# Gate and up pairs of a feed-forward layer in 512-column matmuls, with other PSUM banks and a gate loop that spans three chunks

## The chip, the cores and the metric

The kernel runs on one core of one Trainium2 chip. The metric is the device time of one execution in microseconds (us). The engines of the core are named as in the profile: PE is TensorE's matmul side and PEld its weight load, DVE is VectorE, ACT is ScalarE, POOL is GpSimd, SP is SyncE, whose queue issues the weight transfers. PSUM has eight banks of 512 f32 columns on 128 partitions. Matmuls write it, and DVE and ACT read it.

## The reference, cut to what matters

The program is three transformer layers one after another on 256 tokens of width 1024: one layer with chunked attention and a recurrent branch, one with a gated delta rule, and one with block attention. Each ends in a feed-forward part. That of the first layer is gated, those of the second and third square a ReLU:

```python
D_FF = ((8 * D_MODEL // 3 + 255) // 256) * 256        # 2816
...
        hn = rmsnorm(h, norm_ffn_g[l])
        gu = hn @ w_ffn_in[l]                          # 1024 x 5632
        g, up = jnp.split(gu, 2, axis=-1)
        h = h + (jax.nn.silu(g) * up) @ w_ffn_out[l]
...
def squared_relu_mlp(hn, w_up, w_down):
    return jnp.square(jax.nn.relu(hn @ w_up)) @ w_down  # 1024 x 4096, 4096 x 1024
```

## The kernel before

All activations stay in SBUF with features on partitions and the 256 tokens along the row. All weights come from HBM in **chunks** of 1 MB (128 x 2048 f32, buffer RAW, three slots), 173 in all, and each chunk is used once. The list SEGMENTS gives their order. The segments that matter here are `fi` (22 chunks: gate and up columns of the first feed-forward part, 128 gate columns beside the 128 up columns that belong to them), `fo` (11 chunks, its output rows), `u0` and `u1` (16 chunks each, the up product of the other two), `w0` and `w1` (16 chunks each, their output rows). The prediction calls `fi` the gate stage, `u0` and `u1` the up stages, and `fo`, `w0`, `w1` the row stages.

A product of f32 precision is made of three products of a rounded type (fp32r): each operand is split into a high part and the rest. For a weight chunk, ACT writes the high part WH (`split_hi`, L365) and DVE the rest WL (`split_lo`, L374). For the normed input XH and XL are the two halves of one tile, XHL. Function `product` (L378, L379, L380) then issues WH times XH, WH times XL and WL times XH, each of 256 columns, all into the same 256 columns of PSUM. A chunk of the gate stage is 2 blocks of 128 output features times 8 blocks of 128 input features, so 16 such triples. In the up stages `multiply_wide` (L434, L436) issues two matmuls in place of three: WH times the whole of XHL in 512 columns (XH's result in one half of a bank, XL's in the other), and WL times XH in 256 columns into the second half. Such a chunk holds two banks, those that the table WIDE gives for its place modulo 3. ACT copies the second halves of both banks to SG (L1256), then DVE adds the first halves to them (L1653).

Within the gate stage a chunk takes bank `st.slot` (0, 1 or 2). DVE multiplies its gate half by the norm's row factors RSTD (L1460), ACT applies SiLU (L1127), DVE multiplies by the up half (L1462), which frees the bank, ACT writes the high part HH of the hidden values (L975) and DVE the rest HL (L984). In the row stages all 256 tokens' sums stay in banks 0 to 3 over the whole stage; the matmuls read HH and HL.

Each engine runs its own queue in program order, and semaphores join them: `mm_done` counts finished chunks, `hi_done` and `lo_done` the split ones, `freed` (one for each slot) the read ones, `sg_in`, `sg_done`, `hp_done`, `hh_done`, `hl_done`, `low_out` the steps above. ACT and DVE split chunk c+2 at the start of their turn for chunk c. Before it starts a row stage, PE waits in `banks_free` until every chunk of the stage before it has been read. In the first two chunks of a stage the norm's sums (L563) and rows (L582) are made between the products, and DVE cannot scale anything before it has copied the rows to RSTD (L612).

Of the kernel before, what the change touches and what calls it, by code (L numbers as in the profile page):

```python
# [22 lines left out]
TOK = 256  # L23
# [106 lines left out]
def build(nc, a):  # L130
# [109 lines left out]
    with ExitStack() as ctx:  # L240
# [171 lines left out]
        WIDE = (3, 5, 1)  # L412
# [559 lines left out]
        def hidden_hi(act, st, width):  # L972

            k = slot_of(st, -1)
            act.activation(hid(HH, st, width), HP[:, k, 0:width * TOK].rearrange("p (c t) -> p c t", c=width),  # L975
                           ACT.Copy).then_inc(s_.hh_done, 1)

        def hid(t, st, width):
            return t[:, bass.ds(st.rel_at(-1) * width, width), :]

        def hidden_lo(dve, st, width, earlier):
            k = slot_of(st, -1)
            dve.wait_ge(s_.hh_done, st.local(earlier - 1))
            dve.tensor_tensor(hid(HL, st, width), HP[:, k, 0:width * TOK].rearrange("p (c t) -> p c t", c=width),  # L984
                              hid(HH, st, width).bitcast(F32), ALU.subtract).then_inc(s_.hl_done, 1)
# [3 lines left out]
        def silu_ready(act, st):  # L989
            act.wait_ge(freed[slot_of(st, -1)], st.uses(-1))  # L990
# [7 lines left out]
        def _(act):  # L998
# [118 lines left out]

            def gate(st):
                last = st.i is None and st.j == st.seg.n - 1
                if not last:  # L1120
                    split_hi(act, st)
                if st.i is None and st.j == 0:
                    norm_root(act, 1)
                if st.i is not None or st.j:
                    silu_ready(act, st)
                act.wait_ge(s_.sg_in, st.local())
                act.activation(SG[:, st.slot, 0:TOK], SG[:, st.slot, 0:TOK], ACT.Silu).then_inc(s_.sg_done, 1)  # L1127
                if st.i is not None or st.j:
                    hidden_hi(act, st, 1)
            steps(act, seg["fi"], gate, head=1, tail=1)  # L1130
            end = Step(seg["fi"], seg["fi"].n, None)
            split_hi(act, Step(seg["fi"], seg["fi"].n - 1, None))
            silu_ready(act, end)
            hidden_hi(act, end, 1)
# [110 lines left out]
            def mlp(layer):  # L1245
                sq = squares_ready(16 * layer)

                def up(st):
                    split_hi(act, st)
                    if st.i is None and st.j == 1:  # L1250
                        norm_root(act, 3 + 2 * layer)
                    if st.i is not None or st.j:
                        sq(act, st)
                        hidden_hi(act, st, 2)
                    act.wait_ge(mm_done, st.count())
                    act.activation(two(SG[:, st.slot]), wide_sides(st)[1], ACT.Copy).then_inc(s_.low_out, 1)  # L1256
# [28 lines left out]
        def _(dve):  # L1285
# [166 lines left out]

            def up(st):
                last = st.i is None and st.j == st.seg.n - 1
                if not last:
                    split_lo(dve, st)
# [8 lines left out]
            steps(dve, seg["fi"], up, head=1, tail=1)  # L1465
            split_lo(dve, Step(seg["fi"], seg["fi"].n - 1, None))
            hidden_lo(dve, Step(seg["fi"], seg["fi"].n, None), 1, 0)
# [179 lines left out]
            def mlp(layer):  # L1647
                def square(st):
# [3 lines left out]
                    dve.wait_ge(s_.low_out, st.local(16 * layer))  # L1652
                    dve.tensor_tensor(two(SG[:, st.slot]), two(SG[:, st.slot]), wide_sides(st)[0], ALU.add).then_inc(freed[st.slot], 1)  # L1653
# [43 lines left out]
        def _(pe):  # L1697
# [58 lines left out]
            steps(pe, seg["fi"], times_x(1), head=2)  # L1756
            banks_free(pe, seg["fo"])
# [262 lines left out]
```

## Time and profile before

| | |
|---|---|
| median of 3 runs | 1173.46 us (1173.37 to 1175.54) |
| the profiled execution, its own time | 1173.36 us |
| its span, first to last instruction | 1171.6 us |
| PE busy, share of the span | 97% |
| DVE, ACT busy | 64%, 48% |
| mean granted TensorE clock | 0.996 of full speed |

The profiled execution lies within 0.1 us of the median, and its own time is 1.76 us above its span. Busy time of PE counts a matmul from its start to the modelled end of its pipeline, so it overlaps with the next one. How fast PE really goes is read from the distance between the starts of matmuls.

### The profile page before, as it was taken

To read this page: it belongs to the slowest core of one execution; us is meant where nothing else is said; L and a number is where in the kernel's file an instruction comes from. 1 tells how busy PE (TensorE), PEld (TensorE's weight loads), DVE (VectorE), ACT (ScalarE), POOL (GpSimd) and SP (SyncE) were. 2 spreads that over 40 slices of the span, in tenths; PEclk is the share of its full clock that TensorE was granted. 3 is DMA by queue.
4 is the path that set the end of the run, shared out by engine and by line. 5 is a ranking of instruction groups with operands and counts; after the bars stand their busy time and mean duration, and the time that the engine had idled before them with its cause. 6 is when DMAs were issued, how large, how long until landed. Compare 5 with 4: busy or idle time off the path is not lost.

```text
span 1171.6 us, 21872 instructions
## 1 busy us (share of the span) xinstructions
PE 1132.1 (97%) x8900; PEld 1094.6 (93%) x8900; DVE 755.1 (64%) x922; ACT 564.7 (48%) x727; POOL 213.4 (18%) x222
## 2 busy tenths in 40 slices
PE   6999999999999999998999999999989999999997
PEld 6999889999999999998999898899989999888996
DVE  6647875675666543689886677754467657776333
ACT  6446557445444433565734555543345446554331
POOL 1995003202000000155572020000030002000001
PEclk9999999999999999999999999999999999999999
DMA  9665343654565465344500256655535445655441
GB/s 293 201 217 166 122 145 106 218 172 153 183 211 179 144 215 180 109 143 150 181 31 2 73 180 184 200 177 188 180 104 189 164 142 179 196 181 180 179 143 36
DMA packets 154948, 187.34 MB, mean 160 GB/s; under 512 B 6496, under 2 KB 143872, under 8 KB 154880
## 3 DMA queue, kind: packets, MB, share of 16 engines
q1 hardware_dynamic: 151312, 184.06, 48.2%
q10 hardware_dynamic: 3568, 2.31, 0.7%
q8 instruction: 50, 0.82, 0.3%
q14 instruction: 18, 0.15, 0.0%
HBM read 185.29 MB, written 1.07 MB: 159 GB/s over the span
## 4 chain that ended last, share of the span: by engine, by line
PE 84%; DVE 9%; issue 3%; ACT 2%; SPq 1%; DMA 1%; POOL 0%; POOLq 0%; DVEq 0%; ACTq 0%
PE PS L378 19%; PE PS L379 19%; PE PS L380 19%; PE PS L434 10%; PE PS L436 5%; DVE WL L374 2%; ACT WH L365 1%; DVE XHL L531 1%; PE PS L1874 1%; PE PS L723 1%; PE PS L1860 1%; PE PS L1801 1%; PE PS L673 1%; DMA RAW<-in_w_in 1%; PE PS L1733 1%
## 5 line engine op out<-in xcount | busy, mean ns | idle before, releaser
L374 DVE TENSOR_TENSOR WL<-RAW,WH 128x2048 fp32r<-128x2048 f32 x171 | 405.3, 2371 | 240.2 <-ACT WH L365 240.2
L365 ACT ACTIVATE WH<-RAW 128x2048 fp32r<-128x2048 f32 x171 | 326.5, 1910 | 242.4 <-PE PS L380 200.2
L378 PE MATMUL PS<-XHL,WH 128*128 128x256 f32 x1184 | 342.4, 289 | 15.1 <-DVE WL L327 6.9
L379 PE MATMUL PS<-XHL,WH 128*128 128x256 f32 x1184 | 336.5, 284 | 0.0
L380 PE MATMUL PS<-XHL,WL 128*128 128x256 f32 x1184 | 336.4, 284 | 0.0
L378 PEld LDWEIGHTS PS<-XHL,WH 128*128 128x128 f32 x1184 | 228.7, 193 | 20.6 <-DVE XHL L531 10.8
L379 PEld LDWEIGHTS PS<-XHL,WH 128*128 128x128 f32 x1184 | 229.0, 193 | 0.3
L380 PEld LDWEIGHTS PS<-XHL,WL 128*128 128x128 f32 x1184 | 228.6, 193 | 0.0
L378 PE MATMUL PS<-HH,WH 128*128 (+1 forms) x688 | 195.0, 283 | 4.3 <-DVE SG L1653 2.8
L379 PE MATMUL PS<-HL,WH 128*128 (+1 forms) x688 | 194.7, 283 | 0.0
L380 PE MATMUL PS<-HH,WL 128*128 (+1 forms) x688 | 194.7, 283 | 0.0
L434 PE MATMUL PS<-XHL,WH 128*128 128x512 f32 x512 | 178.4, 395 | 0.0
L436 PE MATMUL PS<-XHL,WL 128*128 128x256 f32 x512 | 142.0, 277 | 0.0
L378 PEld LDWEIGHTS PS<-HH,WH 128*128 128x128 f32 x688 | 132.1, 192 | 5.2 <-DVE SG L1653 3.5
L380 PEld LDWEIGHTS PS<-HH,WL 128*128 128x128 f32 x688 | 132.1, 192 | 0.0
L379 PEld LDWEIGHTS PS<-HL,WH 128*128 128x128 f32 x688 | 132.1, 192 | 0.0
L434 PEld LDWEIGHTS PS<-XHL,WH 128*128 128x128 f32 x512 | 96.0, 188 | 22.2
L642 POOL TENSOR_TENSOR H<-H,XN 128x512 f32<-128x512 f32 x12 | 15.9, 1329 | 528.3 <-DVE XN L629 528.0
L436 PEld LDWEIGHTS PS<-XHL,WL 128*128 128x128 f32 x512 | 96.2, 188 | 0.0
L378 PE MATMUL PS<-OH,WH 128*128 128x256 f32 x192 | 54.4, 283 | 0.0
L380 PE MATMUL PS<-OH,WL 128*128 128x256 f32 x192 | 54.3, 283 | 0.0
L379 PE MATMUL PS<-OL,WH 128*128 128x256 f32 x192 | 54.3, 283 | 0.0
(292 smaller groups left out, 1537.4 us busy)
## 6 DMA issues: line engine op xcount, KB each, us to landing
RAW<-in_mlp_w_up SPq DMA_DIRECT2D x32, 1024.0 KB, 5.5
RAW<-in_mlp_w_down SPq DMA_DIRECT2D x32, 1024.0 KB, 4.9
RAW<-in_w_in SPq DMA_DIRECT2D x26, 1024.0 KB, 5.1
RAW<-in_w_ffn_in_pairs SPq DMA_DIRECT2D x22, 1024.0 KB, 5.1
RAW<-in_dn_w_in SPq DMA_DIRECT2D x16, 1024.0 KB, 5.7
RAW<-in_mb_w_in SPq DMA_DIRECT2D x12, 1024.0 KB, 5.2
RAW<-in_w_ffn_out SPq DMA_DIRECT2D x11, 1024.0 KB, 4.9
RAW<-in_w_attn_out SPq DMA_DIRECT2D x4, 1024.0 KB, 5.1
```

Of the source, the lines that this page charges most:

```text
L365: act.activation(WH[:, k], RAW[:, k], ACT.Copy).then_inc(hi_done, 1)
L374: dve.tensor_tensor(WL[:, k], RAW[:, k], WH[:, k].bitcast(F32), ALU.subtract).then_inc(lo_done, 1)
L378: pe.matmul(out, wh, xh, start=start, stop=False, skip_group_check=True)
L379: pe.matmul(out, wh, xl, start=False, stop=False, skip_group_check=True)
L380: return pe.matmul(out, wl, xh, start=False, stop=stop, skip_group_check=True)
L434: pe.matmul(out.rearrange("p (e t) -> p e t", e=2), h[:, k, part], XHL[:, :, k], start=(k == 0), stop=False, skip_group_check=True)
L436: mm = pe.matmul(out[:, TOK:512], l[:, k, part], XH[:, k], start=False, stop=(k == KB - 1), skip_group_check=True)
L531: ins = dve.scalar_tensor_tensor(out=XL[:, j], in0=H[:, j], scalar=weight(m, j), in1=XH[:, j].bitcast(F32), op0=ALU.mult, op1=ALU.subtract)
L642: ins = pool.tensor_tensor(hb, hb, XN[:, 2 * b:2 * b + 2, :], ALU.add)
L673: mm = pe.matmul(PS[:, 3 + e, P:384], q[:, P:TOK], k[:, 0:TOK], start=True, stop=True)
L723: mm = pe.transpose(PS[:, 5 + e, P * b:P * b + P], PR[:, e, P * b:P * b + P], IDENT[:])
L1733: mm = pe.matmul(PS[:, 3 + j % 2, r * TOK:(r + 1) * TOK], WRI[:, r, j], XN[:, j], start=True, stop=True)
```

## The change

Four edits are made together. The gate stage calls `multiply_wide`. WIDE changes from (3, 5, 1) to (4, 2, 6), so a chunk whose place in its segment is 0, 1 or 2 modulo 3 takes banks 4 and 5, 2 and 3, or 6 and 7; the norm's sums and rows of the gate and up stages go to banks 0 and 1. `banks_free` becomes `rows_banks_free`, which waits for the last chunk of the stage before that used a bank under 4. In the gate stage ACT copies the second halves (`low_half`, L992), DVE adds the first ones (`add_halves`, L997) and scales in SBUF (L1478); SiLU (L1129) and the product with the up half (L1470) are done for the chunk before, and the split of the hidden values for the chunk before that. The constants that count earlier chunks in shared semaphores grow by the gate stage's 22.

```diff
-        WIDE = (3, 5, 1)
+        WIDE = (4, 2, 6)
...
-        def banks_free(pe, sg):
-
-            for k in range(SLOTS):
-                pe.wait_ge(freed[k], uses_upto(sg, k) - sum(1 for c in range(sg.first, sg.first + sg.n) if c % SLOTS == k))
+        def rows_banks_free(pe, wide):
+
+            c = max(wide.first + j for j in range(wide.n) if WIDE[j % SLOTS] < 4)
+            pe.wait_ge(freed[c % SLOTS], c // SLOTS + 1)
...
         def sums_bank(m):
-            return 0 if m in (3, 5) else 4
+            return 0 if m in (1, 3, 5) else 4
 
         def rows_bank(m):
-            return 7 if m in (3, 5) else 5
+            return 1 if m in (1, 3, 5) else 5
...
+        def low_half(act, st):
+
+            act.wait_ge(mm_done, st.count())
+            act.activation(two(SG[:, st.slot]), wide_sides(st)[1], ACT.Copy).then_inc(s_.low_out, 1)
+
+        def add_halves(dve, st, earlier):
+
+            dve.wait_ge(s_.low_out, st.local(earlier))
+            dve.tensor_tensor(two(SG[:, st.slot]), two(SG[:, st.slot]), wide_sides(st)[0], ALU.add).then_inc(freed[st.slot], 1)
...
+            def silu_of(st):
+
+                k = slot_of(st, -1)
+                act.wait_ge(s_.sg_in, st.local(-1))
+                act.activation(SG[:, k, 0:TOK], SG[:, k, 0:TOK], ACT.Silu).then_inc(s_.sg_done, 1)
+
+            def hidden_of(st):
+                act.wait_ge(s_.hp_done, st.local(-2))
+                hidden_hi(act, st, 1, 2)
+
             def gate(st):
-                last = st.i is None and st.j == st.seg.n - 1
-                if not last:
-                    split_hi(act, st)
+                split_hi(act, st)
                 if st.i is None and st.j == 0:
                     norm_root(act, 1)
-                if st.i is not None or st.j:
-                    silu_ready(act, st)
-                act.wait_ge(s_.sg_in, st.local())
-                act.activation(SG[:, st.slot, 0:TOK], SG[:, st.slot, 0:TOK], ACT.Silu).then_inc(s_.sg_done, 1)
-                if st.i is not None or st.j:
-                    hidden_hi(act, st, 1)
...
+                low_half(act, st)
+                if st.i is not None or st.j >= 1:
+                    silu_of(st)
+                if st.i is not None or st.j >= 2:
+                    hidden_of(st)
...
+            def gated(st):
+
+                k = slot_of(st, -1)
+                dve.wait_ge(s_.sg_done, st.local(-1))
+                dve.tensor_tensor(HP[:, k, 0:TOK], SG[:, k, TOK:512], SG[:, k, 0:TOK], ALU.mult).then_inc(s_.hp_done, 1)
...
-                dve.wait_ge(mm_done, st.count())
-                dve.tensor_tensor(SG[:, st.slot, 0:TOK], PS[:, st.slot, 0:TOK], RSTD[:], ALU.mult).then_inc(s_.sg_in, 1)
-                dve.wait_ge(s_.sg_done, st.local())
-                dve.tensor_tensor(HP[:, st.slot, 0:TOK], PS[:, st.slot, TOK:512], SG[:, st.slot, 0:TOK], ALU.mult).then_inc(freed[st.slot], 1)
-                if st.i is not None or st.j:
-                    hidden_lo(dve, st, 1, 0)
...
+                add_halves(dve, st, 0)
+                dve.wait_ge(freed[st.slot], st.uses())
+                dve.tensor_tensor(SG[:, st.slot, 0:TOK], SG[:, st.slot, 0:TOK], RSTD[:], ALU.mult).then_inc(s_.sg_in, 1)
+                if st.i is not None or st.j >= 1:
+                    gated(st)
+                if st.i is not None or st.j >= 2:
+                    hidden_lo(dve, st, 1, 0, 2)
...
-            steps(pe, seg["fi"], times_x(1), head=2)
-            banks_free(pe, seg["fo"])
+            steps(pe, seg["fi"], times_x_wide(1), head=3)
+            rows_banks_free(pe, seg["fi"])
...
-                banks_free(pe, w)
+                rows_banks_free(pe, seg[f"u{layer}"])
```

On PE, at the end of the gate stage, these rows stood before (PS is PSUM; the first three are the last triple of the stage, the next the first of the row stage):

```order
L378 MATMUL PS<-XHL,WH 128x256
L379 MATMUL PS<-XHL,WH 128x256
L380 MATMUL PS<-XHL,WL 128x256
L378 MATMUL PS<-HH,WH 128x256 [waits lo_done,freed2,hl_done,freed1,freed0]
L379 MATMUL PS<-HL,WH 128x256
L380 MATMUL PS<-HH,WL 128x256
```

In the changed kernel the same place reads:

```order
L434 MATMUL PS<-XHL,WH 128x512
L436 MATMUL PS<-XHL,WL 128x256
L378 MATMUL PS<-HH,WH 128x256 [waits hl_done,lo_done,freed2]
L379 MATMUL PS<-HL,WH 128x256
L380 MATMUL PS<-HH,WL 128x256
```

Three 256-column matmuls became one of 512 and one of 256, and two of the waits on `freed` are gone; the one that is left is for chunk 19 of the gate stage, whose slot is 2. In the up stages the matmuls are the same as before, and the wait that is left is for chunk 13.

On DVE, one turn of the gate stage's loop was, from the split of a weight chunk to the next one:

```order
L374 TENSOR_TENSOR WL<-RAW,WH 128x2048 [waits hi_done]
L1459 REGISTER_ALU
L1460 TENSOR_TENSOR SG<-PS,RSTD 128x256 [waits mm_done]
L1461 REGISTER_ALU
L1462 TENSOR_TENSOR HP<-PS,SG 128x256 [waits sg_done]
L983 REGISTER_ALU
L984 ISA [waits hh_done]
L984 TENSOR_TENSOR HL<-HP,HH 128x256
```

It is now:

```order
L374 TENSOR_TENSOR WL<-RAW,WH 128x2048 [waits hi_done]
L996 REGISTER_ALU
L997 TENSOR_TENSOR SG<-SG,PS 128x512 [waits low_out]
L1477 REGISTER_ALU
L1478 TENSOR_TENSOR SG<-SG,RSTD 128x256 [waits freed0]
L1469 REGISTER_ALU
L1470 TENSOR_TENSOR HP<-SG 128x256 [waits sg_done]
L983 REGISTER_ALU
L984 ISA [waits hh_done]
L984 TENSOR_TENSOR HL<-HP,HH 128x256
```

One instruction of 512 columns is new (L997), and what was one chain on one chunk now works on three: L997 and L1478 on chunk c, L1470 on c-1, L984 on c-2.

On ACT, at the start of the gate stage, from the split of its chunk 2 to that of its chunk 3, these rows stood before:

```order
L365 ACTIVATE WH<-RAW 128x2048 [waits mm_done,raw_in0]
L576 ACT_TABLE_LOAD
L576 ACTIVATE SDC<-PS,EPSC 128x2 [waits sum_done]
L1127 ACT_TABLE_LOAD
L1127 ACTIVATE SG<-SG 128x256 [waits sg_in]
L107 UNCONDITIONAL_BRANCH
L107 ISA
L364 ISA [waits raw_in1]
L365 ACTIVATE WH<-RAW 128x2048 [waits mm_done]
```

In the changed kernel:

```order
L365 ACTIVATE WH<-RAW 128x2048 [waits mm_done,raw_in0]
L576 ACT_TABLE_LOAD
L576 ACTIVATE SDC<-PS,EPSC 128x2 [waits sum_done]
L992 ACTIVATE SG<-PS 128x512 [waits mm_done]
L365 ACTIVATE WH<-RAW 128x2048 [waits mm_done,raw_in1]
L992 ACTIVATE SG<-PS 128x512 [waits mm_done]
L1129 ACT_TABLE_LOAD
L1129 ACTIVATE SG<-SG 128x256 [waits sg_in]
```

The split of chunk 3 (the second L365) no longer stands behind the first SiLU, but behind the first copy of second halves.

## Rows read from the trace of the kernel before

**Rows 1.** The page's granted TensorE clock in 40 slices.
```profile
PEclk9999999999999999999999999999999999999999
```

**Rows 2.** Busy time by stretch: the gate stage, the first up stage.
```profile
core 0: us, PE busy (x) PEld busy (x) DVE busy (x) ACT busy (x) POOL busy (x), PEclk, DMA share, GB/s
276.40:403.84 127.44, 127.44 (x1064) 127.38 (x1062) 76.50 (x88) 57.07 (x68) 5.44 (x3) 1.00 0.55 181
680.00:769.60 89.60, 89.60 (x520) 78.24 (x518) 66.56 (x66) 48.97 (x50) 5.43 (x3) 1.00 0.59 188
```

**Rows 3.** PE's timeline in the gate stage: start, duration, line; 22 triples apart.
```profile
276.41 0.28 PE L378 MATMUL PS<-XHL,WH 128*128 128x256 f32 x1
...
284.33 0.28 PE L378 MATMUL PS<-XHL,WH 128*128 128x256 f32 x1
```

**Rows 4.** PE's timeline in the first up stage; first and last 18 pairs apart.
```profile
699.57 0.39 PE L434 MATMUL PS<-XHL,WH 128*128 128x512 f32 x1
699.80 0.27 PE L436 MATMUL PS<-XHL,WL 128*128 128x256 f32 x1
...
705.81 0.39 PE L434 MATMUL PS<-XHL,WH 128*128 128x512 f32 x1
```

**Rows 5.** PE's timeline where each of the three row stages begins.
```profile
403.72 0.28 PE L380 MATMUL PS<-XHL,WL 128*128 128x256 f32 x1
405.53 0.36 PE L378 MATMUL PS<-HH,WH 128*128 128x256 f32 x1 [1.53 <-issue]
...
769.48 0.28 PE L436 MATMUL PS<-XHL,WL 128*128 128x256 f32 x1
771.16 0.39 PE L378 MATMUL PS<-HH,WH 128*128 128x256 f32 x1 [1.41 <-DVE SG L1653]
...
1065.39 0.28 PE L436 MATMUL PS<-XHL,WL 128*128 128x256 f32 x1
1067.08 0.39 PE L378 MATMUL PS<-HH,WH 128*128 128x256 f32 x1 [1.41 <-DVE SG L1653]
```

**Rows 6.** DVE's timeline there: last reads of a bank, next split.
```profile
405.00 0.42 DVE L1462 TENSOR_TENSOR HP<-PS,SG 128x256 f32<-128x256 f32 x1 [0.54 <-ACT SG L1127]
...
770.42 0.69 DVE L1653 TENSOR_TENSOR SG<-SG,PS 128x512 f32<-128x512 f32 x1 [1.45 <-ACT SG L1256]
...
774.82 2.29 DVE L374 TENSOR_TENSOR WL<-RAW,WH 128x2048 fp32r<-128x2048 f32 x1 [1.11 <-ACT WH L365]
```

**Rows 7.** ACT's timeline at the first up stage's end.
```profile
769.79 0.60 ACT L1256 ACTIVATE SG<-PS 128x512 f32<-128x512 f32 x1 [2.36 <-PE PS L436]
```

**Rows 8.** DVE's timeline, one turn of the gate loop.
```profile
318.06 2.29 DVE L374 TENSOR_TENSOR WL<-RAW,WH 128x2048 fp32r<-128x2048 f32 x1 [1.26 <-ACT WH L365]
320.27 0.42 DVE L1460 TENSOR_TENSOR SG<-PS,RSTD 128x256 f32<-128x256 f32 x1
321.17 0.43 DVE L1462 TENSOR_TENSOR HP<-PS,SG 128x256 f32<-128x256 f32 x1 [0.48 <-ACT SG L1127]
321.60 0.43 DVE L984 TENSOR_TENSOR HL<-HP,HH 128x256 f32 x1
```

**Rows 9.** ACT's timeline, one turn of the gate loop.
```profile
320.72 0.42 ACT L1127 ACTIVATE SG<-SG 128x256 f32<-128x256 f32 x1 [2.69 <-DVE SG L1460]
321.05 0.40 ACT L975 ACTIVATE HH<-HP 128x256 f32 x1
321.35 1.90 ACT L365 ACTIVATE WH<-RAW 128x2048 fp32r<-128x2048 f32 x1
```

**Rows 10.** DVE's timeline, then ACT's, at the gate stage's start.
```profile
288.79 0.42 DVE L612 COPY RSTD<-PS 128x256 f32<-128x256 f32 x1 [2.63 <-PE PS L582]
291.96 2.29 DVE L374 TENSOR_TENSOR WL<-RAW,WH 128x2048 fp32r<-128x2048 f32 x1 [1.38 <-ACT WH L365]
...
285.70 0.26 ACT L576 ACTIVATE SDC<-PS,EPSC 128x2 f32<-128x2 f32 x1 [3.83 <-PE PS L563]
```

**Rows 11.** PE's timeline, the first matmul of the gate stage's chunk 3.
```profile
294.33 0.36 PE L378 MATMUL PS<-XHL,WH 128*128 128x256 f32 x1
```

More of the change, by code:

```diff
@@ L969, in _, with hidden_hi, hid, hidden_lo @@
             add_rows(pool, seg["w1"])
-        def hidden_hi(act, st, width):
-            k = slot_of(st, -1)
-            act.activation(hid(HH, st, width), HP[:, k, 0:width * TOK].rearrange("p (c t) -> p c t", c=width),
+        def hidden_hi(act, st, width, back=1):
+            k = slot_of(st, -back)
+            act.activation(hid(HH, st, width, back), HP[:, k, 0:width * TOK].rearrange("p (c t) -> p c t", c=width),
                            ACT.Copy).then_inc(s_.hh_done, 1)
[L978 to L985, printed above, removed]
-        HBASE = {"fi": 0, "u0": 22, "u1": 38}
-        def silu_ready(act, st):
-            act.wait_ge(freed[slot_of(st, -1)], st.uses(-1))
+        def hid(t, st, width, back):
+            return t[:, bass.ds(st.rel_at(-back) * width, width), :]
+        def hidden_lo(dve, st, width, earlier, back=1):
+            k = slot_of(st, -back)
+            dve.wait_ge(s_.hh_done, st.local(earlier - back))
+            dve.tensor_tensor(hid(HL, st, width, back), HP[:, k, 0:width * TOK].rearrange("p (c t) -> p c t", c=width),
+                              hid(HH, st, width, back).bitcast(F32), ALU.subtract).then_inc(s_.hl_done, 1)
+        HBASE = {"fi": 0, "u0": 22, "u1": 38}
+        def low_half(act, st):
[4 more added lines that the diff above has]
+            dve.tensor_tensor(two(SG[:, st.slot]), two(SG[:, st.slot]), wide_sides(st)[0], ALU.add).then_inc(freed[st.slot], 1)
         def squares_ready(earlier):
@@ L1116, in _ @@
             residual("wo", 1)
+            def silu_of(st):
[5 more added lines that the diff above has]
+                hidden_hi(act, st, 1, 2)
             def gate(st):
-                last = st.i is None and st.j == st.seg.n - 1
-                if not last:
-                    split_hi(act, st)
+                split_hi(act, st)
                 if st.i is None and st.j == 0:
                     norm_root(act, 1)
-                if st.i is not None or st.j:
-                    silu_ready(act, st)
-                act.wait_ge(s_.sg_in, st.local())
-                act.activation(SG[:, st.slot, 0:TOK], SG[:, st.slot, 0:TOK], ACT.Silu).then_inc(s_.sg_done, 1)
-                if st.i is not None or st.j:
-                    hidden_hi(act, st, 1)
[L1130 to L1134, printed above, removed]
+                low_half(act, st)
[3 more added lines that the diff above has]
+                    hidden_of(st)
+            steps(act, seg["fi"], gate, head=2)
+            silu_of(Step(seg["fi"], seg["fi"].n, None))
+            hidden_of(Step(seg["fi"], seg["fi"].n, None))
+            hidden_of(Step(seg["fi"], seg["fi"].n + 1, None))
             def row_chunks(w, m):
@@ L1254, in up @@
                         hidden_hi(act, st, 2)
-                    act.wait_ge(mm_done, st.count())
-                    act.activation(two(SG[:, st.slot]), wide_sides(st)[1], ACT.Copy).then_inc(s_.low_out, 1)
+                    low_half(act, st)
                 u = seg[f"u{layer}"]
@@ L1451, in _ @@
             residual("wo", 1)
+            def gated(st):
+                k = slot_of(st, -1)
+                dve.wait_ge(s_.sg_done, st.local(-1))
+                dve.tensor_tensor(HP[:, k, 0:TOK], SG[:, k, TOK:512], SG[:, k, 0:TOK], ALU.mult).then_inc(s_.hp_done, 1)
             def up(st):
-                last = st.i is None and st.j == st.seg.n - 1
-                if not last:
-                    split_lo(dve, st)
+                split_lo(dve, st)
                 if st.i is None and st.j == 0:
                     norm_scale(dve, ch, 1)
-                dve.wait_ge(mm_done, st.count())
-                dve.tensor_tensor(SG[:, st.slot, 0:TOK], PS[:, st.slot, 0:TOK], RSTD[:], ALU.mult).then_inc(s_.sg_in, 1)
-                dve.wait_ge(s_.sg_done, st.local())
-                dve.tensor_tensor(HP[:, st.slot, 0:TOK], PS[:, st.slot, TOK:512], SG[:, st.slot, 0:TOK], ALU.mult).then_inc(freed[st.slot], 1)
-                if st.i is not None or st.j:
-                    hidden_lo(dve, st, 1, 0)
-            steps(dve, seg["fi"], up, head=1, tail=1)
-            split_lo(dve, Step(seg["fi"], seg["fi"].n - 1, None))
-            hidden_lo(dve, Step(seg["fi"], seg["fi"].n, None), 1, 0)
+                add_halves(dve, st, 0)
[5 more added lines that the diff above has]
+                    hidden_lo(dve, st, 1, 0, 2)
+            steps(dve, seg["fi"], up, head=2)
+            gated(Step(seg["fi"], seg["fi"].n, None))
+            hidden_lo(dve, Step(seg["fi"], seg["fi"].n, None), 1, 0, 2)
+            hidden_lo(dve, Step(seg["fi"], seg["fi"].n + 1, None), 1, 0, 2)
             row_chunks(seg["fo"], 2)
@@ L1651, in square @@
                         norm_scale(dve, ch, 3 + 2 * layer)
-                    dve.wait_ge(s_.low_out, st.local(16 * layer))
-                    dve.tensor_tensor(two(SG[:, st.slot]), two(SG[:, st.slot]), wide_sides(st)[0], ALU.add).then_inc(freed[st.slot], 1)
+                    add_halves(dve, st, HBASE[f"u{layer}"])
                     if st.i is not None or st.j:
```

2 lines of the change are left out of this document (1 added, 1 removed).

## The prediction

> **What bounds the kernel now.** I read the granted clock first: it stands at the top of its scale in all 40 slices [rows 1], so nothing below is a matter of the clock. Then the busy time by stretch. In the gate stage and in the up stage PE is busy for the whole stretch, DVE for 76.5 of 127.4 us and 66.6 of 89.6 us, ACT for less, and the DMA engines for 0.55 and 0.59 [rows 2]. So PE is the bound there, and what counts is the distance between the starts of its matmuls. In the gate stage 22 triples take from 276.41 to 284.33, 0.360 us each, or 0.120 us a matmul [rows 3]; 16 triples make a chunk of 5.76 us. In the up stage 18 pairs take from 699.57 to 705.81, 0.3467 us each, 0.23 of it behind the wide matmul [rows 4]; 16 pairs make a chunk of 5.547 us.
>
> Third, PE's timeline at the seams between stages. At the start of each row stage PE stands still [rows 5]. The next matmul could come 0.12 us after the last one: 403.84, 769.60, 1065.51. It comes at 405.53, 771.16 and 1067.08, so 1.69, 1.56 and 1.57 us are lost. The first is put down to issue, the others to DVE's L1653. But DVE's last read of a bank ends at 405.42 and 771.11 [rows 6], 0.11 and 0.05 us ahead of PE's start. All three are the same wait: `banks_free` holds the row stage until the last chunk before it has been read.
>
> **Edit 1: pairs in the gate stage.** It has 22 chunks, 352 pairs in place of 352 triples. The stretch of 127.44 us holds 352 x 0.360 = 126.72 and 0.72 for the norm's small matmuls and the slower matmul after each of them. The up stage, with the same small matmuls, holds 256 x 0.3467 = 88.76 and 0.84. The new gate stage should take 352 x 0.3467 + 0.84 = 122.88 us, 4.56 less. The same pair form on the same tiles is in the trace, 256 times in this stretch, with the clock at 1.00 [rows 2], so I take its price unchanged. As bounds: nothing gained at all (pairs as slow as triples), and at best 352 x 0.0133 = 4.7.
>
> The Trainium skill, "TensorE: Matmul & The Clock Gate", section "Back-to-back issue gap", speaks against this edit: a warm matmul is followed after its columns at 2.4 GHz and about 2.5 ns more. By that, 256 columns take 109 ns and 512 take 216, a triple 327.5, a pair 325.0, and the edit gives 352 x 2.5 ns = 0.9 us. The trace does not agree: 120 ns for 256 columns and 0.23 us for 512 in this kernel, so more than 2.5 ns is saved with each matmul less. The measurement decides.
>
> **Edit 2: the banks.** A gate stage's last chunk (21) and an up stage's last chunk (15) have place 0 modulo 3 and use banks 4 and 5, which the row stages do not touch. The wait that is left is for chunk 19 or 13, read two turns earlier. So the three stalls go: 1.69 + 1.56 + 1.57 = 4.82 us. What is late next? The row stage's first matmul also waits for WL of its first chunk and for the first hidden values. Both were made at least one turn before. The first thing made later is WL of its third chunk. In the up stage's seam it ends at 774.82 + 2.29 = 777.1 [rows 6], and is needed two chunks of 5.76 us after 769.60, at 781.1: 4.0 us spare. I count each seam at 0; the bounds are 0 and the stall that stands there today.
>
> **Edit 3: the gate loop of ACT and DVE.** It must turn in 5.55 us or less. DVE's work in a turn: the split 2.29, the add over 512 columns 0.69 [rows 6], the scaling 0.42, the product 0.43, the hidden rest 0.43 [rows 8]: 4.26 us. ACT's: the split 1.90, SiLU 0.42, the high part 0.40 [rows 9], the copy of 512 columns 0.60 [rows 7]: 3.32 us. Both fit if they don't wait in a ring, so I walk one turn. Let T be the start of a chunk's last matmul. ACT's copy starts at T + 0.31 (769.48 to 769.79 [rows 5, 7]) and ends at T + 0.91; SiLU of the chunk before to T + 1.33, the high part of the one before that to T + 1.73, the next split to T + 3.63. DVE starts its add at T + 0.94, and add, scaling, product and hidden rest end by T + 2.9. It waits for ACT's split until T + 3.63, and ends its own at T + 5.92, half a microsecond ahead of the next copy, which ends at T + 6.46. PE needs that WL, three chunks on, at T + 0.12 + 2 x 5.55 = T + 11.2: 5.3 us spare. The loop is hidden behind PE. Today the round trip to SiLU stops DVE for 0.48 us in each turn [rows 8]; that wait was hidden too, so its removal gives nothing.
>
> At the end of the gate stage ACT drains three chunks ahead of the split for the row stage's third chunk. The last scaling ends at T + 2.05, the last SiLU at T + 2.5, ACT's high part of chunk 20 at T + 2.9. DVE's last product ends at T + 3.3, ACT's last high part at T + 3.7, its split at T + 5.6, DVE's at T + 7.9. PE needs it at T + 0.12 + 11.52 = T + 11.6: 3.7 us spare. Cost 0.
>
> **The start of the gate stage** is the tightest place. Today WL of chunk 3 ends at 291.96 + 2.29 = 294.25 [rows 10], and PE takes it up at 294.33 [rows 11]: 0.08 us to spare. In the new order PE gets there 3 x 0.21 sooner, at 293.7. DVE copies the rows 2 x 0.21 sooner, at 288.37 to 288.79, adds until 289.5, scales until 289.9, and splits until 292.2. WH is ready for it: ACT has the norm's root by 285.96 at the latest [rows 10], then 0.60 and 1.90 make 288.5. So 1.5 us are spare, more than today, because the split no longer stands behind the first SiLU. Cost 0; if a table load of ACT or a DMA came between, at most about 1 us, once.
>
> **The seams into the gate and up stages.** Chunk 0 takes banks 4 and 5, chunk 1 banks 2 and 3, and the norm's sums go to bank 0, all of which the residual's reads have freed before the last piece of the normed input exists. No wait is added there. SP's queue keeps its order; each fetch waits for the DVE split of three chunks before, which ends early as shown, and the DMA engines carried 188 GB/s at the pace of pairs in the up stage [rows 2].
>
> **The sum.** 4.56 + 4.82 = 9.38 us. The profiled execution has 1171.6 us of span and 1.76 around it, 1173.36 in all; minus 9.38 is 1163.98. It stands 0.1 us from the median, so I say 1164.0 us. Everything is on PE's own path and every later stage follows PE, so I let it come through whole.
>
> **The rivals.**
> - *The seams keep a stall.* The first stall is put down to issue, not to DVE, and a row stage starts with matmuls of other code and tiles. If the 4.82 us stay under another name, the time is 1173.4 - 4.6 = 1168.8. Against it: PE starts within 0.11 us of DVE's read in both seams shown. Chance 0.05.
> - *Pairs gain nothing here*, and the seams give their part: 1173.4 - 4.8 = 1168.6. It would need a cause in this stage alone, since the same tiles and form run at 0.3467 us later on. Chance 0.03. This is how the skill's rule would decide, near enough: with its 0.9 us, 1167.7.
> - *The loop becomes the bound: slower.* If ACT and DVE waited for each other through the whole turn, it would last up to 4.26 + 3.32 = 7.58 us, and the stage 22 x (7.58 - 5.76) = 40 us longer, 1173.4 + 40 - 4.8 = 1208.6. It decides against the change as soon as a turn is over 5.76 + 4.82 / 22 = 5.98 us. For it speaks that a turn now has one handover more, the copy. Against it: the walk above has each of them met before it is asked for, and 5.3 us of lead at PE. Chance 0.04.
> - *No change worth measuring:* a turn between 5.87 and 5.98 us, or several stalls at the start of the stage. Chance 0.03.
> - *The forecast*, all parts as computed: 0.85.
>
> **How the numbers follow.** About 0.2% (2.3 us) is what a measurement of this kernel can tell from no change. The forecast and the first two rivals are faster by more than that: 0.93. Same 0.03, slower 0.04. The forecast's own spread is small: 0.3 us more if the slower first matmul after each stall goes too, 1 us less for the start of the stage, and about 1 us for the run itself, since the three runs shown differ by 2. From 1162.5 to 1166 it should hold nearly all of its 0.85. The range reaches to 1167, where the start of the stage and one kept seam would lie together.
>
> **What the profile would show.** In the gate stage pairs 0.347 us apart and a stage of 122.9 us; at the row stages' starts distances of 0.12 us in place of 1.8; in the gate loop DVE waiting for ACT's WH (about 0.7 us) and for ACT's copy (about 0.5), never PE for DVE. DVE's busy time grows by 22 x 0.69 = 15 us and ACT's by 22 x 0.60 = 13 us, with no effect. I am wrong if PE shows idle time ahead of L434 in the gate stage, or if the first L378 of a row stage still waits over a microsecond.

## The result and the profile after

The changed kernel takes 1163.19 us (median of 4 runs, 1161.67 to 1163.79), the kernel before beside it 1173.45 us (4 runs, 1173.37 to 1175.54). The ratio is 0.9903, with a 95% interval of 0.9887 to 0.9919. Against the 1173.46 us of the prediction that is 1162.1 us, 1.9 under the forecast and 0.4 under the low end of its range. The quotient of the two medians is 0.9913, or 1163.2 us; the interval of the ratio, 1160.2 to 1164.0 us, holds both values. The profiled execution took 1162.69 us.

PE's gate stage answers to [rows 2] and [rows 3]. The windows of the changed kernel (gate stage, first up stage):

```profile
core 0: us, PE busy (x) PEld busy (x) DVE busy (x) ACT busy (x) POOL busy (x), PEclk, DMA share, GB/s
275.50:398.36 122.86, 122.86 (x712) 107.44 (x711) 89.52 (x108) 68.53 (x88) 5.44 (x3) 1.00 0.58 188
672.80:762.34 89.54, 89.54 (x520) 78.30 (x519) 66.56 (x66) 48.96 (x50) 5.43 (x3) 1.00 0.59 188
```

The stage lasts 122.86 us where 122.88 were forecast. DVE's busy time in it grew from 76.5 to 89.5 us and ACT's from 57.1 to 68.5, and PE is busy throughout. PE's timeline in the changed kernel, 22 pairs apart inside the stage, and then where each row stage begins (start, duration, line; against [rows 5]):

```profile
329.38 0.40 PE L434 MATMUL PS<-XHL,WH 128*128 128x512 f32 x1
...
337.01 0.40 PE L434 MATMUL PS<-XHL,WH 128*128 128x512 f32 x1
...
398.26 0.28 PE L436 MATMUL PS<-XHL,WL 128*128 128x256 f32 x1
398.38 0.28 PE L378 MATMUL PS<-HH,WH 128*128 128x256 f32 x1
...
762.24 0.28 PE L436 MATMUL PS<-XHL,WL 128*128 128x256 f32 x1
762.36 0.28 PE L378 MATMUL PS<-HH,WH 128*128 128x256 f32 x1
...
1056.45 0.28 PE L436 MATMUL PS<-XHL,WL 128*128 128x256 f32 x1
1056.57 0.28 PE L378 MATMUL PS<-HH,WH 128*128 128x256 f32 x1
```

22 pairs take 7.63 us, 0.3468 each. The three stalls are gone: the row stage's first matmul starts 0.12 us after the last of the stage before, and it lasts 0.28 us, as any other, where it lasted 0.36 and 0.39 behind a stall. DVE's loop in the changed kernel, from one split to the next (against [rows 8]):

```profile
307.33 2.29 DVE L374 TENSOR_TENSOR WL<-RAW,WH 128x2048 fp32r<-128x2048 f32 x1 [0.60 <-ACT WH L365]
...
310.46 0.69 DVE L997 TENSOR_TENSOR SG<-SG,PS 128x512 f32<-128x512 f32 x1 [0.83 <-ACT SG L992]
311.18 0.42 DVE L1478 TENSOR_TENSOR SG<-SG,RSTD 128x256 f32<-128x256 f32 x1
311.52 0.42 DVE L1470 TENSOR_TENSOR HP<-SG 128x256 f32<-128x256 f32 x1
311.86 0.41 DVE L984 TENSOR_TENSOR HL<-HP,HH 128x256 f32 x1
312.88 2.29 DVE L374 TENSOR_TENSOR WL<-RAW,WH 128x2048 fp32r<-128x2048 f32 x1 [0.60 <-ACT WH L365]
```

A turn is 5.55 us, PE's own pace. DVE waits 0.83 us for ACT's copy and 0.60 for WH. PE's timeline has no wait for DVE ahead of any L434 of the stage.

### Where the 9.7 us come from, and what lies outside

PE's timeline gives four lengths (us); the last column is the start of the gate stage, ahead of which the change touches nothing:

| kernel | gate stage and its seam | up stage and seam, twice | gate stage's start to the last row of matmuls | gate stage's start |
|---|---|---|---|---|
| before | 129.12 | 91.14, 91.14 | 885.89 | 276.41 |
| changed | 122.86 | 89.57, 89.58 | 876.15 | 275.52 |

The three stretches are 311.40 and 302.01 us long: 9.39 us less, where the sum said 9.38. The three stretches behind them lose 0.08, 0.15 and 0.12: the slow first matmul of each row stage is no longer in them. Together that is 9.74 us (885.89 to 876.15, with rounding). The other 0.9 us of difference between the two executions lies ahead of the gate stage, where the programs are the same.

### The profile page after: what moved, and what is told of

Its sections match the earlier page's. It is cut to its first block, busy times and chain, and to the rows that moved or that the text cites. A ratio compares the mean times of both kernels' runs of the same rounds, so it can differ in the third digit from the quotient of the medians.

```text
span 1161.0 us, 21202 instructions
## 1 busy us (share of the span) xinstructions
PE 1126.1 (97%) x8548; PEld 1074.3 (93%) x8548; DVE 767.9 (66%) x944; ACT 575.7 (50%) x749; POOL 213.3 (18%) x222
## 4 chain that ended last, share of the span: by engine, by line
PE 84%; DVE 9%; issue 2%; ACT 2%; DMA 1%; SPq 0%; POOL 0%; DVEq 0%; POOLq 0%; ACTq 0%
PE PS L434 17%; PE PS L378 16%; PE PS L379 16%; PE PS L380 16%; PE PS L436 9%; DVE WL L374 2%; ACT WH L365 1%; DVE XHL L531 1%; PE PS L1892 1%; PE PS L1878 1%; PE PS L723 1%; PE PS L1819 1%; PE PS L1751 1%; DVE QKV L1500 1%; DMA RAW<-in_w_in 1%
## 5 line engine op out<-in xcount | busy, mean ns | idle before, releaser
L365 ACT ACTIVATE WH<-RAW 128x2048 fp32r<-128x2048 f32 x171 | 326.8, 1912 | 238.6 <-PE PS L380 196.1
L434 PE MATMUL PS<-XHL,WH 128*128 128x512 f32 x864 | 300.9, 395 | 0.0
L378 PE MATMUL PS<-XHL,WH 128*128 128x256 f32 x832 | 242.5, 291 | 14.9 <-DVE WL L327 6.6
L379 PE MATMUL PS<-XHL,WH 128*128 128x256 f32 x832 | 237.1, 285 | 0.0
L434 PEld LDWEIGHTS PS<-XHL,WH 128*128 128x128 f32 x864 | 162.1, 188 | 37.5
L378 PEld LDWEIGHTS PS<-XHL,WH 128*128 128x128 f32 x832 | 161.3, 194 | 20.0 <-DVE XHL L531 10.5
L379 PEld LDWEIGHTS PS<-XHL,WH 128*128 128x128 f32 x832 | 161.3, 194 | 0.3
L992 ACT ACTIVATE SG<-PS 128x512 f32<-128x512 f32 x54 | 32.3, 599 | 119.6 <-PE PS L436 119.6
L997 DVE TENSOR_TENSOR SG<-SG,PS 128x512 f32<-128x512 f32 x54 | 37.1, 686 | 55.8 <-ACT SG L992 55.7
```

The costliest lines, as they stand in the source:

```text
L365: act.activation(WH[:, k], RAW[:, k], ACT.Copy).then_inc(hi_done, 1)
L378: pe.matmul(out, wh, xh, start=start, stop=False, skip_group_check=True)
L379: pe.matmul(out, wh, xl, start=False, stop=False, skip_group_check=True)
L434: pe.matmul(out.rearrange("p (e t) -> p e t", e=2), h[:, k, part], XHL[:, :, k], start=(k == 0), stop=False, skip_group_check=True)
```

## The experiments

### Both kernels a second time: is the part ahead of the gate stage the change's?

The kernel before and the changed kernel, as they are.

> The kernel before, unchanged, run once more. Theory A (the forecast's sum of 9.4 us is complete, and the rest of the measured difference is the scatter of the program's first 30 us from one execution to the next): the time is 1173.4 us again, but the first matmul of the gate stage, at 276.41 us in the profile of before and at 275.52 in that of the changed kernel, lands elsewhere by some tenths to 1.5 us, and from that matmul to the end the span is 895.2 us as before. Theory B (the change itself brings the 0.9 us ahead of the gate stage): that matmul starts at 276.4 us within 0.1.

> The changed kernel, unchanged, in five rounds. Theory A: 9.4 us faster, ratio 0.9920, with single runs scattering over 2 us; from the first matmul of the gate stage to the end 885.5 us as in its first profile, wherever that matmul starts. Theory B: 10.3 us faster or more, ratio 0.9912 or less, and the matmul starts at 275.5 us again.

Measured, beside runs of the kernel before on the same chip (1174.5 us): the repeat of before 1175.33 us, ratio 1.0006 (0.9995 to 1.0017); the changed kernel 1165.23 us, ratio 0.9922 (0.9907 to 0.9937). From the gate stage's start to the last row of matmuls the two profiles again differ by 9.74 us (885.9, 876.15). That is theory A. The gate stage of the changed kernel did start at 275.5 us again, as theory B had it, but that is chance: other kernels of this study with the same code ahead of it start it up to 4.3 us later. The gate stage's start lay at 276.91 and 275.49 us, and in all twelve profiles of this study between 274.81 and 279.75. Part of this scatter is the granted clock, as windows of the first 130 us show: a norm with the product behind it, and a stretch of 63 matmuls. First the kernel before:

```profile
26.20:41.00 14.80, 14.72 (x123) 14.72 (x124) 11.12 (x13) 5.24 (x3) 12.06 (x11) 1.00 0.72 227
120.00:129.20 9.20, 9.16 (x63) 8.04 (x63) 7.41 (x18) 4.54 (x11) 0.00 (x0) 0.81 0.38 120
```

The changed kernel (its first profile), the same instructions:

```profile
25.40:41.60 16.20, 16.18 (x123) 16.18 (x124) 11.28 (x11) 5.75 (x3) 13.35 (x13) 0.89 0.67 214
120.60:128.30 7.70, 7.64 (x63) 7.01 (x63) 7.43 (x19) 4.54 (x11) 0.00 (x0) 1.00 0.42 137
```

The same work takes 14.8 us at a granted clock of 1.00 and 16.2 at a mean of 0.89; 7.7 us at 1.00 and 9.2 at a mean of 0.81. These means hide a short stretch at half clock (1.2 of 2.4 GHz). In the kernel before, a narrower window shows it:

```profile
120.40:123.78 3.38, 3.38 (x17) 2.40 (x16) 2.19 (x7) 2.44 (x3) 0.00 (x0) 0.50 0.90 303
```

In the first profile of the changed kernel the window from 26.92 to 30.32 us has 0.50 too. Ahead of the one at 120.40 us PE had stood still for 1.89 us, and it stands still for as long at the same place of the changed kernel, where the clock stays at 1.00. The first changed profile has the one slow and the other fast, the kernel before the other way round, and the repeat of the changed kernel has both fast. In the first pair of profiles the clock's two parts cancel (+1.4, -1.5) and 0.8 of the 0.9 us are there before the first of the two windows (25.4 for 26.2); in the second pair the 1.4 us are the one window, 9.2 and 7.7. Over the twelve profiles the gate stage starts at 274.8 and 275.5 us where no such stretch lies ahead of it (two profiles), at 275.5 to 276.9 with one (six), and at 278.3 to 279.8 with two (four). The page showed none of this: a slice is 29 us long, and its digit 9 is anything from 0.9 up.

### Triples in the gate stage, all else as changed

```diff
-                pe.matmul(out.rearrange("p (e t) -> p e t", e=2), h[:, k, part], XHL[:, :, k], start=(k == 0), stop=False,
-                          skip_group_check=True)
+                pe.matmul(out[:, 0:TOK], h[:, k, part], XH[:, k], start=(k == 0), stop=False, skip_group_check=True)
+                pe.matmul(out[:, TOK:512], h[:, k, part], XL[:, k], start=False, stop=False, skip_group_check=True)
```

> The changed kernel, but each pair of the gate stage is issued as three matmuls of 256 columns into the same two banks; ACT, DVE, the banks and the waits stay as changed. If the pair form alone is worth 352 x 0.0133 us, the gate stage is 127.4 us long, 4.6 us longer than changed, and the time is 1167.9 us. Rival, that the new loop or the banks shorten the stage and not the form: under 1 us slower than changed. The skill's isolated gap (2.5 ns a matmul) would give 0.9 us.

Measured: 1169.72 us, ratio 0.9961 (0.9945 to 0.9978); the stage 127.36 us against 122.86, so the pairs are worth 4.50 us, 12.8 ns for each of the 352 matmuls saved. PE's timeline of this kernel:

```profile
349.75 0.28 PE L440 MATMUL PS<-XHL,WL 128*128 128x256 f32 x1
349.87 0.28 PE L435 MATMUL PS<-XHL,WH 128*128 128x256 f32 x1
349.99 0.28 PE L436 MATMUL PS<-XHL,WH 128*128 128x256 f32 x1
350.11 0.28 PE L440 MATMUL PS<-XHL,WL 128*128 128x256 f32 x1
```

Matmuls of 256 columns start 0.120 us apart; the same banks, copies and loop stand behind them, so nothing else in the change made this stage faster. The Trainium skill, "TensorE: Matmul & The Clock Gate", section "Back-to-back issue gap", gives an isolated matmul at the full clock about 2.5 ns beside its columns; an estimate from that figure is 0.9 us for the stage. The same section gives other distances for a stream of weight loads and matmuls, about 81 ns with 128 columns and about 131 ns with 512, and the prediction left these out. The trace agrees with neither: at a granted clock of 1.00 it has 120 ns for 256 columns and 347 ns for a pair of 512 and 256.

### The banks alone, in the kernel before

```diff
-        WIDE = (3, 5, 1)
+        WIDE = (4, 2, 6)
...
-                banks_free(pe, w)
+                u = seg[f"u{layer}"]
+                c = max(u.first + j for j in range(u.n) if WIDE[j % SLOTS] < 4)
+                pe.wait_ge(freed[c % SLOTS], c // SLOTS + 1)
```

The norm's rows of the last two layers go to bank 1. The gate stage and its seam stay as they were.

> The kernel before with the new table of banks and the shorter wait in the two up stages only; the gate stage and its seam are as before. The seams into the last two row stages should be 0.12 us in place of 1.68 and 1.69, and the time 3.1 us less: 1170.3 us. Rival, that another wait stands in the seam: 0 to 3 us less. Theory B of an uncounted gain: more than 3.1 us less outside these seams.

Measured: 1171.35 us, ratio 0.9972 (0.9961 to 0.9983), 3.3 us less. Both up stages with their seams take 89.57 and 89.58 us, 3.13 less together. PE's timeline at the first:

```profile
773.95 0.28 PE L436 MATMUL PS<-XHL,WL 128*128 128x256 f32 x1
774.06 0.28 PE L378 MATMUL PS<-HH,WH 128*128 128x256 f32 x1
```

### The whole change, but PE waits for the last chunk's read at each seam

```diff
-            c = max(wide.first + j for j in range(wide.n) if WIDE[j % SLOTS] < 4)
+            c = wide.first + wide.n - 1
             pe.wait_ge(freed[c % SLOTS], c // SLOTS + 1)
```

> The changed kernel, but each row stage waits again until the last chunk of the stage before it is read; banks stay as changed. The last read of the gate stage is now DVE's add, not its product, and ends 1.63 us after the last matmul's start. So each of the three seams should cost 1.5 to 1.6 us, 4.7 in all: 4.7 us slower than changed, 1168 us. Rival, that the stall went because of the banks and not of the wait: same as changed.

Measured: 1170.6 us, ratio 0.9975 (0.996 to 0.999). PE's timeline of this kernel at the gate stage's end:

```profile
399.00 0.28 PE L436 MATMUL PS<-XHL,WL 128*128 128x256 f32 x1
400.69 0.38 PE L378 MATMUL PS<-HH,WH 128*128 128x256 f32 x1 [1.41 <-DVE SG L997]
```

At all three seams the distance is 1.69 us in place of 0.12: 1.57 each, 4.7 in all, and the stretch behind each is longer by 0.1. The median is 2.6 us over the 1168 expected, and the profile is 6.5 us longer than the changed kernel's from the gate stage on: beside the 5.0 at and behind the seams it has 1.5 us more in a stretch at a granted clock of 0.50, from 652.1 to 655.5 us, which the changed kernel's profiles don't have. The banks are those of the change; only the moment at which PE may go on differs. So the stall is the handover from PE's last matmul over ACT's copy to DVE's add, and the other banks help because the read that PE then waits for is two turns old.

### The gate loop on one chunk

The pairs and the banks stay; copy, add, scaling, SiLU and product all work on chunk c, and the hidden split on c-1, as in the kernel before.

```diff
             def silu_of(st):
-                k = slot_of(st, -1)
-                act.wait_ge(s_.sg_in, st.local(-1))
+                k = st.slot
+                act.wait_ge(s_.sg_in, st.local())
...
-                act.wait_ge(s_.hp_done, st.local(-2))
-                hidden_hi(act, st, 1, 2)
+                act.wait_ge(s_.hp_done, st.local(-1))
+                hidden_hi(act, st, 1)
...
             def gated(st):
-                k = slot_of(st, -1)
-                dve.wait_ge(s_.sg_done, st.local(-1))
+                k = st.slot
+                dve.wait_ge(s_.sg_done, st.local())
```

> The changed kernel with pairs, but SiLU, the product and the hidden high part follow in the same turn, as before: one chain over one chunk. The prediction said that the wait for SiLU is hidden and that its removal gives nothing; by that, the time is that of the changed kernel, plus up to 1 us once for chunk 3. Rival, the ring: before, the turn of the ring took 5.22 us where PE did not bound it (DVE's add of 0.69 us now comes into it, so 5.95), against 5.55 us of PE. Then DVE falls back 0.4 us a turn, the lead of 4 us is used up after ten turns, and the gate stage is 4 to 8 us longer.

Measured: 1174.11 us, ratio 1.0003 (0.9987 to 1.0019): the whole gain is gone. The gate stage with its seam takes 131.46 us, 8.6 more than in the changed kernel, and the row stage behind it 1.2 more. DVE's timeline of this kernel, one turn:

```profile
314.63 2.29 DVE L374 TENSOR_TENSOR WL<-RAW,WH 128x2048 fp32r<-128x2048 f32 x1 [1.28 <-ACT WH L365]
316.84 0.68 DVE L997 TENSOR_TENSOR SG<-SG,PS 128x512 f32<-128x512 f32 x1
317.56 0.42 DVE L1475 TENSOR_TENSOR SG<-SG,RSTD 128x256 f32<-128x256 f32 x1
318.46 0.42 DVE L1467 TENSOR_TENSOR HP<-SG 128x256 f32<-128x256 f32 x1 [0.48 <-ACT SG L1129]
318.91 0.42 DVE L984 TENSOR_TENSOR HL<-HP,HH 128x256 f32 x1
320.58 2.29 DVE L374 TENSOR_TENSOR WL<-RAW,WH 128x2048 fp32r<-128x2048 f32 x1 [1.24 <-ACT WH L365]
```

PE's timeline where it waits for that split:

```profile
322.51 0.28 PE L436 MATMUL PS<-XHL,WL 128*128 128x256 f32 x1
323.00 0.50 PE L434 MATMUL PS<-XHL,WH 128*128 128x512 f32 x1 [0.21 <-DVE WL L374]
```

A turn is 5.95 us. DVE is busy for 4.2 of it and waits for ACT twice, with ACT waiting for DVE in between: WL, add, scaling (DVE), SiLU, HH, WH (ACT), and WL again. That is a ring, and it holds whatever PE does. The kernel before had it too, without the add: from WL at 318.06 [rows 8] to the end of WH at 321.35 + 1.90 = 323.25 [rows 9] are 5.19 us, under the 5.76 of three matmuls. With the add's 0.69 it is 5.88, over the 5.55 of pairs. The 8.6 us are more than the 4 to 8 that this ring was expected to cost, because PE has no lead of 4 us where the stage begins: it waits 0.81 us for the WL of chunk 3 already, and 19 turns of 0.4 us follow.

### The gate loop over two chunks

SiLU and the product on c-1 as changed, the hidden split on c-1 in place of c-2.

```diff
-                act.wait_ge(s_.hp_done, st.local(-2))
-                hidden_hi(act, st, 1, 2)
+                act.wait_ge(s_.hp_done, st.local(-1))
+                hidden_hi(act, st, 1)
...
-                if st.i is not None or st.j >= 2:
-                    hidden_lo(dve, st, 1, 0, 2)
+                if st.i is not None or st.j >= 1:
+                    hidden_lo(dve, st, 1, 0)
```

> The changed kernel, but the gate loop spans two chunks in place of three: SiLU and the product are for the chunk before, and the hidden high part and rest follow in the same turn. The loop over one chunk measured a turn of 5.95 us, of which DVE waited 0.48 for SiLU. Taking that wait out leaves a ring of 5.47 us, just under PE's 5.55. So the gate stage should be 122.9 us as changed and the time the same as changed, 1164 us. Rival, that the third chunk is needed: a turn of 5.6 us or more, and a gate stage over 123.5 us.

Measured: 1176.01 us, ratio 1.002 (1.0004 to 1.0036); the gate stage 132.36 us. My expectation fell. DVE's timeline, one turn:

```profile
320.31 2.29 DVE L374 TENSOR_TENSOR WL<-RAW,WH 128x2048 fp32r<-128x2048 f32 x1 [1.24 <-ACT WH L365]
322.52 0.68 DVE L997 TENSOR_TENSOR SG<-SG,PS 128x512 f32<-128x512 f32 x1
323.24 0.42 DVE L1477 TENSOR_TENSOR SG<-SG,RSTD 128x256 f32<-128x256 f32 x1
323.58 0.42 DVE L1469 TENSOR_TENSOR HP<-SG 128x256 f32<-128x256 f32 x1
324.69 0.43 DVE L984 TENSOR_TENSOR HL<-HP,HH 128x256 f32 x1 [0.69 <-ACT HH L975]
326.38 2.29 DVE L374 TENSOR_TENSOR WL<-RAW,WH 128x2048 fp32r<-128x2048 f32 x1 [1.26 <-ACT WH L365]
```

And ACT's:

```profile
324.12 0.42 ACT L975 ACTIVATE HH<-HP 128x256 f32 x1 [3.05 <-DVE HP L1469]
324.44 1.90 ACT L365 ACTIVATE WH<-RAW 128x2048 fp32r<-128x2048 f32 x1
```

The ring is still closed, at another place, and 0.12 us longer (every third turn 0.32). ACT's split now stands behind HH, HH behind this turn's product, the product behind the add and the scaling: 320.31 to 326.38 is 6.07 us. Only with the hidden split two chunks back does ACT ask DVE for nothing that DVE makes in the same turn.

### How much room DVE has: useless multiplications

These two kernels leave nothing out. They add one multiplication of the norm's row factors to each turn of DVE's gate loop, of 768 or 2048 columns, whose result goes to blocks of HL that the gate stage does not use.

```diff
                 if st.i is not None or st.j >= 1:
                     gated(st)
+                    dve.tensor_tensor(HL[:, 22:22 + 3], by_rows(3), by_rows(3), ALU.mult)
```

> The changed kernel with one useless DVE multiplication over 768 columns in each turn of the gate loop but the first, some 0.9 us (rows of 256, 512 and 2048 columns took 0.42, 0.69 and 2.29 us). DVE waits 0.60 + 0.83 = 1.43 us in a turn of the changed kernel, so the extra work should vanish in it: the gate stage 122.9 us as changed. Rival, that DVE's waits are part of a ring and any added work lengthens the turn: up to 0.9 x 20 = 18 us slower.

> The same with 2048 columns, 2.2 us a turn, more than DVE's 1.43 us of waits. A turn is then 4.0 + 2.2 = 6.2 us of DVE work against 5.55 of PE, DVE falls back 0.6 us a turn, and PE starts to wait when the 5.3 us of lead are gone, after nine turns or so: the gate stage 5 to 8 us longer than changed, 128 to 131 us. Rival, no lead: 20 x 0.6 = 12 us longer or more.

Measured, with 768 columns: 1165.32 us, ratio 0.992 (0.9891 to 0.9948), the gate stage 122.85. With 2048: 1180.73 us, ratio 1.0054 (1.0032 to 1.0077), the stage 132.18. DVE's timeline with 2048:

```profile
314.20 2.29 DVE L374 TENSOR_TENSOR WL<-RAW,WH 128x2048 fp32r<-128x2048 f32 x1
...
317.80 2.28 DVE L1481 TENSOR_TENSOR HL<-RSTD 128x2048 fp32r<-128x2048 f32 x1
320.00 0.42 DVE L984 TENSOR_TENSOR HL<-HP,HH 128x256 f32 x1
320.34 2.28 DVE L374 TENSOR_TENSOR WL<-RAW,WH 128x2048 fp32r<-128x2048 f32 x1
```

No wait stands in this turn of 6.14 us: here DVE itself is the bound. PE lost 9.3 us in the gate stage, where 5 to 8 had been expected. The expectation gave PE the lead of 5.3 us that it has in the middle of the stage; where the stage begins the lead is 1.5 us (in the changed kernel WL of chunk 3 ends at 291.45 us and PE begins that chunk at 292.99), and 19 turns that are 0.58 us too long make 11.0 us. Another 5.2 us are lost in the row stage behind it, which neither theory had, and 2.6 further on, where the granted clock of this profile is 0.50 for longer than in the changed kernel's (557.4 to 564.2 and 666.6 to 670.0 us, there 542.3 to 545.7). PE's timeline in the row stage, and the window from 420 us:

```profile
420.60 0.28 PE L380 MATMUL PS<-HH,WL 128*128 x1
423.68 0.38 PE L378 MATMUL PS<-HH,WH 128*128 x1 [2.81 <-DVE WL L374]
```

```profile
420.00:440.00 20.00, 17.20 (x131) 17.00 (x130) 10.05 (x5) 8.53 (x5) 0.00 (x0) 0.91 0.55 209
```

DVE enters the row stage in arrears, WL of its third chunk comes 2.81 us late, and from 424.25 to 427.65 us the matmuls start 0.21 us apart in place of 0.12: the granted clock is 0.50 there, which makes the 0.91 of the whole window. A loop that is slower than PE costs more than its own stage shows.

### More matmuls of fewer columns

In the gate stage WL times XH is issued as two matmuls of 128 columns in place of one of 256: 352 matmuls more, the same columns.

```diff
-                mm = pe.matmul(out[:, TOK:512], l[:, k, part], XH[:, k], start=False, stop=(k == KB - 1),
-                               skip_group_check=True)
+                for q in range(2):
+                    mm = pe.matmul(out[:, TOK + q * P:TOK + (q + 1) * P], l[:, k, part], XH[:, k, q * P:(q + 1) * P], start=False,
+                                   stop=(k == KB - 1), skip_group_check=True)
```

> The changed kernel, but in the gate stage WL times XH is issued as two matmuls of 128 columns in place of one of 256: 352 more matmuls, the same columns. If each matmul costs 13 ns over its columns, the gate stage is 4.7 us longer. By the skill's isolated gap it is 0.9 us longer. Rival, that the weight load of 128 columns sets a floor under a short matmul (it shows 0.188 us, overlapped): more than 4.7 us, since two of 128 columns then take as long as two loads.

Measured: 1204.76 us, ratio 1.0263 (1.0231 to 1.0294); the stage 161.32 us, 38.46 more, 0.109 us for each further matmul. PE's timeline:

```profile
330.42 0.45 PE L434 MATMUL PS<-XHL,WH 128*128 128x512 f32 x1
330.71 0.22 PE L438 MATMUL PS<-XHL,WL 128*128 128x128 f32 x1
330.77 0.27 PE L438 MATMUL PS<-XHL,WL 128*128 128x128 f32 x1
330.88 0.45 PE L434 MATMUL PS<-XHL,WH 128*128 128x512 f32 x1
```

A group lasts 0.458 us, 0.111 more than a pair's 0.347, so the fixed 12.8 ns does not describe what one more matmul costs. The 0.111 us stand in two places: the wide matmul is followed after 0.29 us where it was 0.23, and the two short ones after 0.06 and 0.11, 0.17 together, where the one of 256 columns was followed after 0.12. The weight loads of the two short matmuls, PEld's timeline:

```profile
330.48 0.19 PEld L438 LDWEIGHTS PS<-XHL,WL 128*128 128x128 f32 x1
330.71 0.19 PEld L438 LDWEIGHTS PS<-XHL,WL 128*128 128x128 f32 x1
```

The second load starts only as the first short matmul does. That PE waits for these loads would fit the rows, but no run took the load away from a matmul, so it is argued and not shown.

## Why the prediction was right, and where not

**The sum** held. Edit 1 was put at 4.56 us and measured 4.50 by itself. Edit 2 was put at 4.82 and returned 4.7 when the last read was waited for again; the two up seams alone gave 3.13 of the 3.13 foreseen. The stages with their seams are 9.39 us shorter, for 9.38. The "0.3 us more if the slower first matmul after each stall goes too" belonged into the sum: it came, with 0.35. DVE's and ACT's busy time was to grow by 15 and 13 us and grew by 13.0 and 11.5 in the window of the stage, which holds 20 instructions more of each and not 22.

**The issue row at the first seam** was rightly read as the same wait as the others. With the last read waited for, the wait there is put down to DVE's L997.

**Edit 3, the walk of the turn,** gave DVE waits of "about 0.7 us" for WH and "about 0.5" for the copy; they are 0.60 and 0.83. The start of the gate stage kept its room: WL of chunk 3 ended at 291.45 and PE took it up at 292.99, the 1.5 us to spare that were foreseen.

**"That wait was hidden too, so its removal gives nothing"** was wrong. The round trip to SiLU was hidden behind triples, but with pairs and one more DVE instruction its ring lasts 5.95 us, and the kernel with it is as slow as the kernel before. The step compared the old turn with the old pace; it should have been closed with the new add and held against 5.55. The wait for SiLU by itself is not what counted: the loop over two chunks is rid of it and is no faster. The forecast did not suffer, since it walked the new loop. But the account of what carries the gain did: the edit that was priced at nothing is what lets the 9.7 us of the others come through.

**The Trainium skill's rule against edit 1** would have given 0.9 us by the prediction's estimate; the stage gave 4.50. The rival "pairs gain nothing" is out, and so is "the seams keep a stall". "The loop becomes the bound" was a real danger: the loop over one chunk (a turn of 5.95 us) stands 0.03 us from the 5.98 from which it decides, and the loop over two (6.07) is beyond it.

**The spread of the forecast** is the step that failed, and with it the low end of the range. It rested on "about 1 us for the run itself" and on "nothing below is a matter of the clock". Over the whole study the kernel before ran from 1171.0 to 1179.0 us and the changed one from 1161.7 to 1166.6, and the same code ahead of the gate stage took 274.8 to 279.8 us. The clock is a good part of it: of 70 runs of the kernel before, the 8 with a mean granted clock of 0.997 have a median of 1171.5 us and the 12 with 0.993 one of 1176.0. Three runs that lie within 2 us are no measure of that, nor is a row of 40 nines. The 0.35 us left out of the sum took a part of the 1.5 us between the forecast and that end. The remaining 0.4 us by which the time lies outside are within the scatter, and a time just inside would have been no better a confirmation. Of the two ratios of the changed kernel, the first gives 1162.1 us and the repeat 0.9922 x 1173.46 = 1164.3, so 11.4 and 9.2 us less; their intervals overlap, and what both pairs of profiles show from the gate stage on is 9.74.

What stays open: why the clock falls to half in some executions and not in others (the norm's stretch and the 63 matmuls near 120 us had 1.00 in some profiles and means of 0.89 and 0.81 in others, with the same instructions), and the part of the scatter ahead of 26 us. Nor was another order of ACT's queue tried with a loop over two chunks, so three chunks are shown to be enough, and needed only in this order.

## What to carry to other kernels

Close every ring of handovers between two engines with the change's new instructions in it, and hold it against the new pace of the engine that leads: a wait that is hidden today can be the bound once that engine is faster. Move work back by as many chunks as it takes until neither engine asks for what the other makes in the same turn; one chunk less gave nothing here. Choose the banks so that the last tile before a stage that needs whole banks lies outside them, and take the spread of a forecast from the stretches that the change leaves alone, in more than one profile, with the clock read in windows of a few microseconds. A lead that holds in the middle of a stage has to be read at its start as well.

## What was not expected of the hardware

Issuing 256 columns as two matmuls of 128, each with its own weight load, made a group of 0.347 us one of 0.458, 0.111 us for each further matmul; half of it came behind the 512-column matmul ahead of them. The first matmul behind a stall of over a microsecond lasts 0.38 us where others last 0.28, and the stretch behind each seam was 0.08 to 0.15 us longer for it. The granted clock of one and the same stretch of instructions differed between executions: over 63 matmuls it was 1.00 throughout, or 0.50 for a part of it and 0.81 on average, which is 1.5 us.
